# Turning queries and keys of the mixing layer by 32x32 blocks on VectorE and through DRAM instead of by transposes on TensorE

## The reference

```python
rq, rk, rv, rg, nq, nk, nv, g_ret, g_na = jnp.split(u @ w_in, points, axis=-1)
q = _rotary(heads(rq, RET_QK_DIM), pos)
k = _rotary(heads(rk, RET_QK_DIM), pos) * (RET_QK_DIM ** -0.5)
y = _bidirectional_retention(q, k, heads(rv, RET_V_DIM), decay_fwd, decay_bwd)
...
y_na = _neighborhood_attention(na_heads(nq), na_heads(nk), na_heads(nv), rel_bias) @ w_na_out
```

## Time and profile before

| | |
|---|---|
| median of three runs | 1209.76 us |
| span of the profiled execution, first to last instruction | 1207.9 us |
| TensorE busy | 1197.5 us, 99% |
| VectorE busy | 950.9 us, 79% |
| ScalarE busy | 622.3 us, 52% |
| GpSimd busy | 84.8 us, 7% |
| mixing slots 3 to 25 | from about 213 us on |

### The profile page before, as it was taken

One profiled execution on the slowest core, in us unless ns is written; L12 is line 12 of the kernel. 1 busy time (PEld: TensorE's weight loads), 2 busy tenths in 40 slices (PEclk: granted clock), 3 DMA queues, 4 the chain that ended last, 5 costly groups with the idle time before them and its releaser, 6 DMA issues.

```text
span 1207.9 us, 14813 instructions
## 1 busy us (share of the span) xinstructions
PE 1197.5 (99%) x5798; PEld 983.4 (81%) x5798; DVE 950.9 (79%) x1382; ACT 622.3 (52%) x851; POOL 84.8 (7%) x133
## 2 busy tenths in 40 slices
PE   9999999999999999999999999999999999999997
PEld 7888888888778888888887778888888788888885
DVE  7799868876766689888786668898898878765656
ACT  7445337445774363434465667444446576643441
POOL 2110130000300011000000000000100000000000
PEclk9999999999999999999999999999999999999999
DMA  9999996644645489899566437788856544566640
GB/s 317 347 337 322 307 302 192 218 142 154 203 152 174 152 297 355 309 328 316 172 208 206 139 105 263 271 304 280 309 196 241 192 141 139 177 219 214 188 161 35
DMA packets 145685, 274.31 MB, mean 227 GB/s; under 512 B 6336, under 2 KB 76432, under 8 KB 145616
## 3 DMA queue, kind: packets, MB, share of 16 engines
q1 hardware_dynamic: 127568, 209.73, 51.7%
q0 software_dynamic: 17888, 63.57, 15.4%
q10 hardware_dynamic: 160, 0.07, 0.0%
HBM read 270.41 MB, written 2.93 MB: 226 GB/s over the span
## 4 chain that ended last, share of the span: by engine, by line
PE 94%; DVE 2%; ACT 2%; issue 1%; DVEq 0%
PE ps L532 24%; PE ps L534 24%; PE ps L533 24%; PE ps L865 7%; PE ps L864 3%; PE ps L784 2%; PE ps L732 1%; PE ps L611 1%; ACT hi_w L1194 1%; PE ps L1081 1%; PE ps L738 1%; PE ps L1060 1%; PE ps L942 1%; PE ps L1058 1%; ACT area L1511 1%
## 5 line engine op out<-in xcount | busy, mean ns | idle before, releaser
L1707 DVE TENSOR_TENSOR lo_w<-w_raw,hi_w 128x2048 fp32r<-128x2048 f32 x194 | 440.9, 2286 | 60.9 <-ACT hi_w L1194 60.5
L1194 ACT ACTIVATE hi_w<-w_raw 128x2048 fp32r<-128x2048 f32 x195 | 370.2, 1915 | 51.4 <-DMA w_raw<-in_ffn_w_in 18.6
L532 PE MATMUL ps<-hi_w,xT 128*128 128x512 f32 x848 | 339.4, 400 | 0.0
L534 PE MATMUL ps<-lo_w,xT 128*128 128x512 f32 x848 | 331.3, 391 | 0.0
L533 PE MATMUL ps<-hi_w,xT 128*128 128x512 f32 x848 | 330.7, 390 | 0.0
L532 PEld LDWEIGHTS ps<-hi_w,xT 128*128 128x128 f32 x848 | 159.4, 188 | 36.3 <-issue 4.9
L532 PE MATMUL ps<-hi_w,hT_hi 128*128 128x512 f32 x480 | 188.5, 393 | 0.0
L534 PEld LDWEIGHTS ps<-lo_w,xT 128*128 128x128 f32 x848 | 159.2, 188 | 34.3
L534 PE MATMUL ps<-lo_w,hT_hi 128*128 128x512 f32 x480 | 187.1, 390 | 0.0
L533 PE MATMUL ps<-hi_w,hT_lo 128*128 128x512 f32 x480 | 187.0, 390 | 0.0
L533 PEld LDWEIGHTS ps<-hi_w,xT 128*128 128x128 f32 x848 | 159.6, 188 | 30.8
(11 more groups left out here) (321 smaller groups left out, 1152.1 us busy)
## 6 DMA issues: line engine op xcount, KB each, us to landing
w_raw<-in_ffn_w_in SPq DMA_DIRECT2D x86, 512.0 KB
aux<-in_ada_w POOLq DMA_DIRECT2D x34, 1024.0 KB, 7.5
w_raw<-in_mlp_w_up SPq DMA_DIRECT2D x32, 1024.0 KB
w_raw<-in_mlp_w_down SPq DMA_DIRECT2D x32, 1024.0 KB
w_raw<-in_w_mix_in SPq DMA_DIRECT2D x26, 1024.0 KB
w_raw<-in_ffn_w_out SPq DMA_DIRECT2D x22, 1024.0 KB
area<-in_ada_w POOLq DMA_DIRECT2D x14, 1024.0 KB, 5.6
w_raw<-in_moba_w_in SPq DMA_DIRECT2D x12, 1024.0 KB
```

The source lines that it names most:

```text
L532: pe.matmul(dst, lhs_hi, rhs_hi, start=start, stop=False)
L534: return pe.matmul(dst, lhs_hi, rhs_lo, start=False, stop=stop)
L1194: act.activation(hi_w[:, ring_slot(u), :], w_raw[:, ring_slot(u), :], ACT.Copy).then_inc(w_hi, 1)
L1707: vec.tensor_tensor(lo_w[:, ring_slot(u), :], w_raw[:, ring_slot(u), :], hi_w[:, ring_slot(u), :].bitcast(F32), ALU.subtract).then_inc(w_l ...
```

## The change

After the change, DVE turns a stage itself, as 32x32 blocks within the partitions' four groups of 32, in one instruction per stage (slots 2, 4, 6 and 8), into a new buffer `turned`. POOL then writes that buffer to DRAM (128 partitions x 4 KB), waits until it is there, and reads it back with four transfers of 32 partitions each, so that block (a, b) lands where block (b, a) was. TensorE has no transposes of these four any more, and DVE no copies. Where the result lies, the tokens of a head are no longer next to each other: the view `"p (n c t) -> p c t n"` has 8 floats, 32 bytes, from one token to the next.

```diff
+        head_dram = nc.dram_tensor("head_scratch", (4, P, 1024), F32, kind="Internal").ap()
-        qT = part(0, 1024, 4)
-        kT = part(1024, 1024, 4)
+        mix_heads = [part(off, 1024) for off in (0, 1024, 4096, 5120)]
+        qT, kT, nqT, nkT = [v.rearrange("p (n c t) -> p c t n", c=4, t=NT) for v in mix_heads]
+        turned = part(9216, 1024)
...
             def ret_scores(h):
-                pe.wait_ge(headT_out, 3)
+                pe.wait_ge(head_landed, 2 * 64)
...
-                    mm = pe.matmul(ps[:, off:off + SEQ], kT[:, h, m * P:(m + 1) * P], qT[:, h, :],
+                    mm = pe.matmul(ps[:, off:off + SEQ], kT[:, h, m], qT[:, h],
...
             def ret_outputs(h):
-                pe.wait_ge(headT_out, 4)
...
             def na_scores_of(pair):
-                pe.wait_ge(headT_out, 4)
+                pe.wait_ge(head_landed, 4 * 64)
...
-                        mm = pe.matmul(ps[:, off:off + SEQ], nqT[row, pair, t * P:(t + 1) * P], nkT[row, pair, :],
+                        mm = pe.matmul(ps[:, off:off + SEQ], nqT[row, pair, t], nkT[row, pair],
...
-                    if half == 1 and 1 <= b <= 4:
-                        n = b - 1
-                        if n < 2:
-                            pe.wait_ge(rot_done, n + 1)
-                        else:
-                            pe.wait_ge(proj_out, PB_MIX + n + 1)
-                            pe.wait_ge(headT_out, n - 1)
-                        transposes(stage[n % 2], 0, 4, 2 * (n % 2) * BANK).then_inc(headT, 1)
-                        if n == 0:
-                            later_vectors_T()
+                    if slot == 3:
+                        pe.wait_ge(rot_done, 1)
+                        later_vectors_T()
...
                 if b in (2, 3):
-                    act.wait_ge(headT, b - 1)
+                    act.wait_ge(head_turned, b - 1)
...
-                if slot in (4, 6, 8, 10):
-                    n = slot // 2 - 2
-                    vec.wait_ge(headT, n + 1)
-                    vec.tensor_copy([qT, kT, nqT, nkT][n], bank(2 * (n % 2), 2).rearrange("p (c n) -> p c n", c=4))\
-                       .then_inc(headT_out, 1)
+                if slot in (2, 4, 6, 8):
+                    n = slot // 2 - 1
+                    vec.wait_ge(proj_out, PB_MIX + n + 1)
+                    if n < 2:
+                        vec.wait_ge(rot_done, n + 1)
+                    if n >= 1:
+                        vec.wait_ge(head_saved, 16 * n)
+                    vec.transpose(turned.rearrange("p (b j c t) -> p t c b j", b=4, j=32, c=4),
+                                  stage[n % 2].rearrange("p t (c b i) -> p t c b i", b=4, i=32)).then_inc(head_turned, 1)
...
-            for h in range(NA_H):
+            for h in range(2):
+                bias_of(h)
+            for n in range(4):
+                pool.wait_ge(head_turned, n + 1)
+                pool.dma_start(head_dram[n], turned).then_inc(head_saved, 16)
+                pool.wait_ge(head_saved, 16 * (n + 1))
+                rows_of = head_dram[n].rearrange("(a i) (b r) -> b i a r", a=4, b=4)
+                for b in range(4):
+                    dst = mix_heads[n][32 * b:32 * b + 32, :].rearrange("p (a r) -> p a r", a=4)
+                    pool.dma_start(dst, rows_of[b]).then_inc(head_landed, 16)
+            for h in range(2, NA_H):
                 bias_of(h)
```

More of the change, by code:

```diff
@@ L260, in two_blocks_kernel @@
         g_na = v_nat
-        nqT = part(4096, 1024, 4)
-        nkT = part(5120, 1024, 4)
         nv = part(6144, 1024, NT)
@@ L327, in two_blocks_kernel @@
         rot_done, headT, headT_out = sem("rot_done"), sem("headT"), sem("headT_out")
+        head_turned, head_saved, head_landed = sem("head_turned"), sem("head_saved"), sem("head_landed")
         mod_landed = [sem("mod_landed0"), sem("mod_landed1")]
@@ L1043, in heads_T @@
                 def heads_T(n):
-                    pe.wait_ge(rot_done, hb - 2 + n + 1)
+                    pe.wait_ge(rot_done, hb + 2 + n + 1)
                     if n >= 1:
@@ L1179, in attention @@
                         modulation_rows_2()
-            attention(S_MOBA, U_MOBA, PB_MOBA, 4, NA_H, CH_MOBA_O, False)
+            attention(S_MOBA, U_MOBA, PB_MOBA, 0, NA_H, CH_MOBA_O, False)
             mlp(S_MLP1, U_MLP1, B_MLP1, T_MLP1)
-            attention(S_DIFF, U_DIFF, PB_DIFF, 8, NA_H + 8, CH_DIFF_O, True)
+            attention(S_DIFF, U_DIFF, PB_DIFF, 4, NA_H + 8, CH_DIFF_O, True)
             mlp(S_MLP2, U_MLP2, B_MLP2, T_MLP2)
@@ L1671, in attention @@
                     act.activation(table_in[:, 2:3], table_in[:, 0:1], ACT.Sqrt)
-            attention(U_MOBA, PB_MOBA, 4, NA_H, CH_MOBA_O, False)
+            attention(U_MOBA, PB_MOBA, 0, NA_H, CH_MOBA_O, False)
             after_ln(S_MOBA, U_MLP1)
@@ L1676, in _ @@
             after_ln(S_MLP1, U_DIFF)
-            attention(U_DIFF, PB_DIFF, 8, NA_H + 8, CH_DIFF_O, True)
+            attention(U_DIFF, PB_DIFF, 4, NA_H + 8, CH_DIFF_O, True)
             after_ln(S_DIFF, U_MLP2)
@@ L2412, in rotate @@
                         vec.wait_ge(ld_tab, 16 * 5)
-                    vec.wait_ge(rot_done, hb - 2 + n)
+                    vec.wait_ge(rot_done, hb + 2 + n)
                     rows = buf.rearrange("p t (h n) -> p t h n", n=HD)
```

## The result

The changed kernel takes 1214.38 us (median of 5 runs, 1214.19 to 1214.45) against 1209.70 for the kernel before on the same chip: 4.7 us slower, a ratio of 1.0038 with a 95% interval of 1.0027 to 1.005. 1206.2 was forecast, with a range up to 1213.5.

The account below looks back on a forecast made before the run. TensorE was taken to bound the kernel, busy 1197.5 of 1207.9 us. Removing transposes saves 3.6 us and all other terms cost nothing: 1209.76 - 3.6 = 1206.2 us, range 1205.4 to 1213.5.

Parts of the forecast that it names:

- Removed from TensorE, 3.6 us: Four groups of eight transposes leave TensorE's queue between 209 and 257 us, saving 3.6 us.
- VectorE, at nothing: Four copies go, four turnings of 1.13 us (at most 2.3) come; cost nothing, hidden by a 12.8 us lead.
- POOL, the DMA queues and the new wait: 4 MB more traffic delays nothing; rq and rk land at 239.3 to 245.7, before the first scores at 246.1.
- The strided products: Retention and neighbourhood passes reading with 32 bytes between tokens: taken as nothing, upper end 7.7 us.
- the strided passes double: Slower rival: retention pays 3.4 us and the neighbourhood 3.9, giving 1213.5 us; chance 0.20.
- The lower price of 3.5: Lower bound of the doubling's cost in the neighbourhood: 3.5 us, eight starts of 0.109 us in each group.

Follow-up runs that it names:

- the version with dense heads and no wait: The changed kernel with each head's tokens dense and head 0's scores asked for at slot 9 instead of 8: 1206.17 us against 1209.89.
- the versions with shorter runs: The changed kernel with tokens dense (DRAM reads in 128-byte runs), 1207.44 us, or 8 bytes apart (256-byte runs), 1207.88 us.
- The last two runs: The kernel before, one projection unit's 24 products reading their moving operand with 16, then 8 bytes between columns: 1215.67 and 1215.12 us against 1210.01.

## Why the prediction was wrong

- **Removed from TensorE, 3.6 us: right.** The first scores moved from 248.85 to 246.25, and the version with dense heads and no wait gains 3.7 us.
- **VectorE, at nothing: right.** The turning took 2.2 us where I took 1.13, within the bounds; from 205 to 360 us the trace has no wait of a matmul for VectorE. A small thing was missed: `later_vectors_T` still waits for the rotation of rq, and with the transposes gone from ahead of it, it starts at 218.62 instead of 218.53.
- **POOL, the DMA queues and the new wait: right for the kernel as it is.** The last of rk's reads landed at 243.3 us, inside the 239.3 to 245.7 that were added up. The 3 us to spare are not much: the versions with shorter runs came late.
- **The strided products, "I take nothing, because the nearest row about the read rate is the projection's": this step failed.** The term is 8.3 us, above its upper end of 7.7. The reasoning was that, if a strided read runs at half the dense rate of the projection, a pass which asks for a column half as often does not notice. But the projection's row shows a dense read by another kind of pass. The last two runs show that the half rate is right for the projection itself, 0.88 to 0.90 ns for each column, and with 8 bytes between tokens the F32 passes hardly notice, as was argued. With 16 or 32 bytes they have no such reserve: they get a column every 1.8 ns.
- **The rival "the strided passes double"** named the mechanism, the place and nearly the price: 1213.5, with 0.20. It priced the passes at 3.4 + 3.9 = 7.3 us, and they cost 8.3. Retention's passes take 2.16 times as long rather than twice (4.0 us), and the neighbourhood's groups cost their whole length once more (4.4 us). The lower price of 3.5, "eight starts of 0.109 us", averaged over passes that start in pairs, and each group paid its full 1.09 us. These are the 0.9 us by which the time lies above the rival, and above the range.
- The sentence from the Trainium skill (Advanced Engine Details and Errata, SBUF Cachelines) was the only evidence that bore on this read directly, and it was right for F32. I weighed it lower than an inference from rows that did not show a strided operand.

Why the F32 passes fall to 1.8 ns at 16 bytes, where F32R stays at 0.90, is open; the runs show that it is so, not by what mechanism.

## What to carry to other kernels

When data takes a new road to TensorE, look at how it lies at the end of the road: a moving operand with one F32 column to 16 or 32 bytes doubled every pass that read it, and here that was worth more than twice what the removed transposes cost. A rate that one kind of instruction reaches on dense data says nothing about the reserve of another kind on strided data; where a rule speaks against the change and no row speaks for it, its case deserves the larger chance. A round trip through DRAM wants a consumer that can be moved back: one slot later cost nothing here, and with it the wait and the spread were gone.

## What the runs showed of the hardware that had not been expected

- A strided stationary operand costs little in this stream, though its load takes 0.33 us instead of 0.19: 1.3 us of 48 passes in the trace, 0.8 in the median. A moving one costs 0.25 us for each F32 pass of 256 columns on 128 partitions, and about as much for each pair of passes on 64.
- F32R products double already at 8 bytes from column to column (0.227 to 0.45 us for 512 columns) and get hardly slower at 16 (0.46).
- VectorE pays for strided writing too: a copy of 128x1024 from PSUM takes 2.07 us with tokens 32 bytes apart, 1.22 with 8 bytes and 1.22 dense, and a turning of as many elements in the memory 2.16 with 32 bytes and 1.24 dense. With 16 bytes, a copy of half as many elements takes 1.07.
- 4 MB more traffic, 285 GB/s instead of 198 from 209 to 257 us, did not make TensorE wait; it is busy for all of the 48 us:

```profile
209.00:257.00 48.00, 48.00 (x204) 38.78 (x203) 42.52 (x47) 24.75 (x22) 8.82 (x16) 1.00 0.87 285
```
